# Gate rows computed beside the first products, one chain for q, k and v, and mLSTM written out with its head norm merged

## What is computed

```
proj = x @ w_in    -> qa ka va oa ia fa qkv_b zb beta_b a_b gate_a gate_b
ha   = mlstm(qa, ka, va, i = ia + b_i, f = fa + b_f)        # 4 heads, q and k 128 wide, v 256 wide
       s = (q k^T) * w,  w = exp(decay + i - running max);  h = (s v) / max(|sum s|, exp(-m))
ha   = h * rsqrt(mean(h*h over 256) + 1e-6) * g             # norm of each head
ha   = ha * sigmoid(oa)
qkv  = silu(causal_conv(qkv_b, 4 taps));  hb = gated_delta(l2norm(q), l2norm(k), v, beta, g)
y    = sigmoid(gate_a) * (ha @ w_a) + sigmoid(gate_b) * (hb' @ w_b)
x    = layernorm(ALPHA * x + y @ w_out);  then a gated feed-forward and a second layernorm
```

## Time and profile before

| | us |
|---|---|
| median of 3 runs (4377.66 to 4385.02) | 4377.89 |
| profiled execution | 4381.01 |
| its span, first to last instruction | 4379.2 |
| PE busy | 3860.3 (88%) |
| DVE busy | 1900.5 (43%) |
| ACT busy | 1234.8 (28%) |
| POOL busy | 238.9 (5%) |
| layer 0: gates to the start of branch_a | 1466.37 to 1715.32 |
| layer 1: the same | 2925.25 to 3172.69 |

### The profile page before, as it was taken

The page is one execution under the profiler, slowest core; times in us unless marked ns, Lnnn a source line. Parts: engine busy times, 40 slices in busy tenths (PEclk is TensorE's granted clock), DMA queues, the critical chain, the costliest instruction groups (busy, mean ns, idle before and its releaser), DMA issues. The chain is left out here.

```text
span 4379.2 us, 52698 instructions
## 1 busy us (share of the span) xinstructions
PE 3860.3 (88%) x20305; PEld 3165.7 (72%) x20305; DVE 1900.5 (43%) x2569; ACT 1234.8 (28%) x1839; POOL 238.9 (5%) x300
## 2 busy tenths in 40 slices
PE   7787999989999587998889989958699888898997
PEld 6656999966888364785887778846387588686886
DVE  3365524335433324375444443332436544544333
ACT  2243212234222322323323232223222323323222
POOL 0000000000000000001330000000100033000000
PEclk9888999979999698997999999988799899998999
DMA  2101222211222111220002122212022100122222
GB/s 106 49 9 39 91 93 87 87 33 58 100 96 96 33 58 39 78 95 20 0 0 85 70 93 95 90 46 77 0 96 91 44 1 0 52 100 70 91 94 83
DMA packets 52158, 279.08 MB, mean 64 GB/s; under 512 B 12081, under 2 KB 15161, under 8 KB 23773
## 3 DMA queue, kind: packets, MB, share of 16 engines
q1 hardware_dynamic: 51986, 276.75, 18.6%
HBM read 274.43 MB, written 2.27 MB: 63 GB/s over the span
## 5 line engine op out<-in xcount | busy, mean ns | idle before, releaser
L317 PE MATMUL ps<-xs,ffn_w 128*128 128x512 f32 x2112 | 484.4, 392 | 29.5 <-DVE xs L561 29.5
L317 PEld LDWEIGHTS ps<-xs,ffn_w 128*128 128x128 f32 x2112 | 399.7, 189 | 114.6 <-issue 31.1
L317 PE MATMUL ps<-u,mlp_w 128*128 128x264 f32 (+1 forms) x2880 | 456.2, 321 | 14.8 <-DVE mlp_w L555 10.0
L317 PEld LDWEIGHTS ps<-u,mlp_w 128*128 128x128 f32 x2880 | 417.2, 190 | 53.4 <-issue 15.5
L317 PE MATMUL ps<-hn,mlp_w 128*128 128x264 f32 (+1 forms) x2304 | 363.7, 320 | 0.0
L317 PEld LDWEIGHTS ps<-hn,mlp_w 128*128 128x128 f32 x2304 | 332.4, 188 | 30.4 <-issue 0.5
L317 PE MATMUL ps<-xs,cv_w 128*128 128x512 f32 x1152 | 268.2, 394 | 13.5 <-DVE xs L561 9.8
L317 PEld LDWEIGHTS ps<-xs,cv_w 128*128 128x128 f32 x1152 | 217.5, 190 | 64.2 <-issue 17.7
L317 PE MATMUL ps<-ff,ffn_w 128*128 128x512 f32 x1056 | 240.0, 389 | 0.0
L355 ACT CAST ffn_w<-raw 128x2048 fp32r<-128x2048 f32 (+1 forms) x74 | 124.0, 1676 | 383.2 <-PE ps L317 343.2
L317 PEld LDWEIGHTS ps<-ff,ffn_w 128*128 128x128 f32 x1056 | 198.2, 188 | 41.2
(11 more groups left out here) (422 smaller groups left out, 5497.3 us busy)
## 6 DMA issues: line engine op xcount, KB each, us to landing
raw<-in_w_ffn_up SPq DMA_DIRECT2D x44, 1024.0 KB, 4.9
raw<-in_w_up SPq DMA_DIRECT2D x32, 1024.0 KB, 4.8
raw<-in_w_down SPq DMA_DIRECT2D x32, 1024.0 KB, 4.8
raw<-in_w_conv SPq DMA_DIRECT2D x24, 1024.0 KB, 4.9
raw<-in_w_ffn_down SPq DMA_DIRECT2D x32, 704.0 KB, 4.0
raw<-in_w_mqk SPq DMA_DIRECT2D x10, 1024.0 KB, 5.7
raw<-in_w_mo SPq DMA_DIRECT2D x8, 1024.0 KB, 4.9
mv_raw<-in_w_mv SPq DMA_DIRECT2D x16, 512.0 KB, 6.2
```

The source lines that it names most:

```text
L317: ins = nc.tensor.matmul(bank(u)[:, h, :], w[:, s, wp, k * g.bw + j * P:k * g.bw + (j + 1) * P], g.xs[:, xp, k, h * n:(h + 1) * n], start= ...
```

## The change

- The gates are no stage of their own. A class `Gates` holds their instructions in portions, which `chain` issues on each engine at fixed places (its new argument `beside`): portion -1 before the first product (on ACT and DVE after the splitting of `x`), portion n behind block n. It uses the odd PSUM banks.
- The gate weights stay in a buffer `gates_w` of their own. They are loaded before the layers for layer 0, and at the start of branch_b for the next layer; between, the buffer serves `delta_rule` as its `u`.
- q, k and v are one chain "mqkv" of 4 + 4 blocks. v is a new kind of product, `tokens`: `xs` is the stationary side and 256 columns of weights move, 384 matmuls of 256 columns instead of 192 of 512. Its weights come in the stream like all others.
- `mlstm` is written out for the four heads with two sets of buffers, in an order in which a head's scores are made ahead. q, k, v and a are read where they lie. It makes the head norm too: PE sums the squares of the undivided numerator, and the scaling is 1 / sqrt(sum/256 + 1e-6 * max(..)^2), so division and norm are one reciprocal. `row_norm` "mn" is gone.
- `xs1` stays until the convolution's chain, which no longer splits `x`.

```diff
-        two = [[("w_mqk", 0)], [("w_mo", 0), ("w_branch_a", 0), ("w_ga", 0)], [("w_conv", 0)],
+        two = [[("w_mqk", 0), ("w_mv", 0)], [("w_mo", 0), ("w_branch_a", 0), ("w_ga", 0)], [("w_conv", 0)],
...
+                        if g.evac == "tokens":
+                            for c in range(2):
+                                for k in range(g.kc):
+                                    for e, (wp, xp) in enumerate(PASSES):
+                                        tok = (2 * j + c) * P
+                                        ins = nc.tensor.matmul(
+                                            bank(u)[:, 0, c * BW:(c + 1) * BW], g.xs[:, xp, k, tok:tok + P],
+                                            w[:, s, wp, k * BW:(k + 1) * BW], start=(k == 0 and e == 0),
+                                            stop=(k == g.kc - 1 and e == 2))
...
+                def rest(g, b, pos):
+                    step(g, b, pos)
+                    if beside is not None and isinstance(b, int):
+                        beside.tensor(pe, g.b0 + b)
```

The portions of `Gates` (new code, shortened):

```diff
+    def tensor(self, pe, n):
+        if n == -1:
+            pe.wait_ge(self.w_in, 16 * (self.layer + 1))
...
+        if n == 3:
+            pe.wait_ge(s["a_done"], 1)
+            pe.wait_ge(s["beta_done"], 1)
+            pe.wait_ge(s["gc_done"], NCH)
...
+        if n >= 4:
+            self.spread(pe, 2 * (n - 4))
+            self.spread(pe, 2 * (n - 4) + 1)
...
+    def scalar(self, act, n):
+        if n == 0:      # tanh, sigmoid
...
+        if n == 1:      # exp, exp, abs, exp, ln, ln
...
+        if n == 3:      # exp, two casts
...
+        if n == 4:      # three small exps
...
+        if 5 <= n < 7:
+            self.copy_spread(act, 2 * (n - 5))
+            self.copy_spread(act, 2 * (n - 5) + 1)
+        if n == 7:
+            for j in range(4, 2 * MH):
+                self.copy_spread(act, j)
...
+    def vector(self, dve, n):
+        if n == -1:     # reads the projection, four operations
...
+        if n == 2:      # all running sums and what lies between them
...
+        if n == 4:      # reads the transposes
```

mLSTM, the order on each engine:

```diff
+                scores(0)
+                scores(1)
+                for i in range(MH):
+                    sums(i)
+                    if 1 <= i < MH - 1:
+                        scores(i + 1)
+                    weights_and_squares(i)
...
+                weights(0)
+                weights(1)
+                for i in range(MH):
+                    act.wait_ge(s["summed"], i + 1)
+                    for j in range(2):
+                        if i:
+                            act.wait_ge(s["sq_summed"], i)
+                        nc.scalar.activation(sq[:, j, :], ps[:, 4 + j, :], ACT.Square).then_inc(s["squared"], 1)
+                        nc.scalar.copy(out[:, 2 * i + j, :], ps[:, 4 + j, :]).then_inc(s["copied"], 1)
+                    act.wait_ge(s["den_summed"], i + 1)
+                    nc.scalar.activation(den[:, i % 2, :], ps[:, 7, :], ACT.Abs).then_inc(s["abs_done"], 1)
+                    act.wait_ge(s["bounded"], i + 1)
+                    nc.scalar.activation(den[:, i % 2, :], den[:, i % 2, :], ACT.Square, scale=(EPS * MDV) ** 0.5).then_inc(s["den_squared"], 1)
+                    if i + 2 < MH:
+                        weights(i + 2)
+                    act.wait_ge(s["added"], i + 1)
+                    nc.scalar.activation(inv[:, i % 2, :], inv[:, i % 2, :], ACT.Sqrt, scale=1.0 / MDV).then_inc(s["rooted"], 1)
...
+                args(0)
+                args(1)
+                weigh(0)
+                weigh(1)
+                for i in range(MH):
+                    if i + 2 < MH:
+                        args(i + 2)
+                    if 1 <= i and i + 1 < MH:
+                        weigh(i + 1)
...
+                    dve.wait_ge(s["rooted"], i + 1)
+                    nc.vector.reciprocal(inv[:, i % 2, :], inv[:, i % 2, :]).then_inc(s["inverted"], 1)
```

And in `second_block`:

```diff
-                        gates(nc, ps, x, a, layer, par, ident, ones, sel, m_rows_b, a_cols, g_rows, cols)
-                        chain(nc, ps, ws, "mqk", [dense("qk", xs, KC, D, "act", dst=qk, func=ACT.Copy)], whole=x)
-                        project_tokens(nc, ps, "mv", xs, [c * P for c in range(NCH)], [P] * NCH, a["w_mv"], [layer * 2, layer * 2 + 1],
-                                       SEQ, [v[:, :, j * SEQ:(j + 1) * SEQ] for j in range(2)])
...
-                            chain(nc, ps, ws, "cv", [dense("cv", xs, KC, 3 * D, "conv", dst=qkv, func=ACT.Silu, taps=par[:, CONV_W:CONV_W + 96])], whole=x)
...
+                                chain(nc, ps, ws, "mqkv", [dense("qk", xs, KC, D, "act", dst=qk, func=ACT.Copy),
+                                                           dense("v", xs, KC, D, "tokens", dst=v)], whole=x, beside=beside)
...
+                        chain(nc, ps, ws, "cv", [dense("cv", xs, KC, 3 * D, "conv", dst=qkv, func=ACT.Silu, taps=par[:, CONV_W:CONV_W + 96])])
...
+                                  beside=NextGates(gates_w, gates_in, a["w_gates"], layer))
```

More of the change, by code:

```diff
@@ L185, in __init__, with chain @@
         self.squares, self.inv, self.ones, self.mean = squares, inv, ones, mean
-def chain(nc, ps, ws, name, gemms, whole=None, gain=None, squares=None, room=None):
+def chain(nc, ps, ws, name, gemms, whole=None, gain=None, squares=None, room=None, beside=None):
     halves, n = gemms[0].halves, gemms[0].n
@@ L271, in enter @@
                     eng.wait_ge(sem, count)
+        if beside is not None:
+            beside.open(st)
         with nc.Block() as block:
@@ L275, in _ @@
             def _(sp):
+                if beside is not None:
+                    beside.sync(sp)
                 for i, g in enumerate(gemms):
@@ L335, in _ @@
                         sum_squares(g, i)
-                    rolled(pe, g.n_blocks - 1, g.unroll, lambda b, pos: step(g, b + 1, pos + 1))
+                    if beside is not None:
+                        beside.tensor(pe, g.b0)
+                    rolled(pe, g.n_blocks - 1, g.unroll, lambda b, pos: rest(g, b + 1, pos + 1))
             @block.scalar
@@ L405, in evacuate @@
                             tile(g, b * g.tpb + j, pos, j)
+                    if beside is not None and isinstance(b, int):
+                        beside.scalar(act, g.b0 + b)
                 g = gemms[0]
@@ L421, in _ @@
                             nc.scalar.activation(sq[:, c % 2, :], whole[:, c, :], ACT.Square).then_inc(x_squared, 1)
+                if beside is not None:
+                    beside.scalar(act, -1)
                 for i, g in enumerate(gemms):
@@ L545, in evacuate @@
                         two_parts(g, b, v)
-                    elif g.evac != "act":
+                    elif g.evac not in ("act", "tokens"):
                         for j in range(g.tpb):
                             tile(g, b * g.tpb + j, pos, j)
+                    if beside is not None and isinstance(b, int):
+                        beside.vector(dve, g.b0 + b)
                 g = gemms[0]
@@ L602, in _ @@
                     nc.gpsimd.memset(eps_col[:, :], EPS).then_inc(eps_set, 1)
+                if beside is not None:
+                    beside.gpsimd(pool)
 def project_tokens(nc, ps, name, xs, starts, sizes, w_dram, w_rows, n, dsts, inv=None):
@@ new lines, in sums @@
+                def sums(i):
+                    for n, c in enumerate(order):
+                        pe.wait_ge(s["weighed"], NCH * i + n + 1)
+                        for j in range(2):
+                            if i and c == 0:
+                                pe.wait_ge(s["squared"], 2 * (i - 1) + j + 1)
+                                pe.wait_ge(s["copied"], 2 * (i - 1) + j + 1)
+                            ins = nc.tensor.matmul(ps[:, 4 + j, c * CHUNK:SEQ], v[:, c, i * MDV + j * P:i * MDV + (j + 1) * P],
+                                                   w[:, i % 2, off[c]:off[c] + width[c]], start=(n == 0), stop=(n == NCH - 1))
+                    ins.then_inc(s["summed"], 1)
@@ new lines, in weights_and_squares @@
+                def weights_and_squares(i):
+                    if i:
+                        pe.wait_ge(s["abs_done"], i)
+                    for c in range(NCH):
+                        ins = nc.tensor.matmul(ps[:, 7, c * CHUNK:SEQ], ones, w[:, i % 2, off[c]:off[c] + width[c]],
+                                               start=(c == 0), stop=(c == NCH - 1))
+                    ins.then_inc(s["den_summed"], 1)
+                    for j in range(2):
+                        pe.wait_ge(s["squared"], 2 * i + j + 1)
+                        ins = nc.tensor.matmul(ps[:, 2 * (i % 2), :], ones, sq[:, j, :], start=(j == 0), stop=(j == 1))
+                    ins.then_inc(s["sq_summed"], 1)
@@ new lines, in weights @@
+                def weights(i):
+                    act.wait_ge(s["arg_ready"], i + 1)
+                    if i >= 2:
+                        act.wait_ge(s["den_summed"], i - 1)
```

(13 more changed lines are left out.)

427 lines of the change are left out of this document (221 added, 206 removed).

## The result

The changed kernel takes 4221.04 us, median of four runs (4214.87 to 4225.07), against 4377.77 for the kernel before in the same comparison: a ratio of 0.9637, 95% interval 0.9620 to 0.9654. The forecast of 4217 is 4 us away, inside case A's own range. The profiled execution took 4219.93.

The account below looks back on a forecast made before the run. PE was taken as bound, waiting in chains of small steps in gates and mLSTM; each layer's stretch becomes 111.4 + 56.5 = 167.9 us, saving 160.7 together, 4381.0 to 4220.3, forecast 4217 (3.1 above median), range 4198 to 4250.

Parts of the forecast that it names:

- case A: Whole kernel: the forecast itself, 4217 us, with its own range 4203 to 4231; chance 0.60.
- E: v's matmuls in the chain: held by weight loads, 0.242 us each, 4309 us in all; chance 0.03.
- F: v's matmuls in the chain: 256 columns run at the fp32 rate, 0.43 us each, 4453 us; chance 0.03.
- Margin (a): Chain, block 2: gates portion 1 on ACT, then block 3's cast and DVE's rest, end 0.7 us in time.
- Margin (b): Chain, block 3: portion 2 on DVE (9.2 us), then v's first rest, ready at 10.8 of 11.2 us.
- (c): Chain: portion 3 on ACT, 3 us, delays v's second block to 8 of 11.2 us, still covered.
- C: Chain: helpers late, 4 us at three blocks and one clock fall a layer, 4245 us; chance 0.10.
- The wait: mLSTM, before head 3's sums: PE waits once, 2.5 us, for ACT's exponentials and root, then DVE's reciprocal and products.
- B: Chain and mLSTM: clock falls seven times a layer, 4248 us, shown by a clock under 0.9; chance 0.14.
- "lp": Before layer 0: early gate-weight transfer stands ahead of the parameters this stage waits for; 1.0 us charged once.
- The 0.6 a layer: Convolution's chain: without splitting its input, PE starts at 1.49 us instead of 2.09, saving 0.6 a layer.
- The place of `xs`: Products reading xs: its new SBUF address might alter their rate, worth 0.8 us a layer over 8 tiles, either way.

Follow-up runs that it names:

- the longer helper: Changed kernel with six more ACT operations of 8 x 512 behind the logarithms, ahead of the cast of block 3; 4236.43 us, 0.9663.
- the padded kernel before: Kernel before with 64 unused bytes ahead of the weight buffers of mqk and branch_a; 4388.8 us, 1.0016.
- gates in front: Changed kernel with all portions of the gates issued ahead of the first product; 4264.88 us, 0.9731.
- the first with `xs1` moved: Changed kernel with 32 unused bytes a partition ahead of xs1, its weights not padded; 4214.34 us, 0.9620.

## Why the prediction was right, point by point

- **The chain, 111.4 forecast, 109.9 measured.** Projection 9.0 (10.1), q and k 45.3 (44.8), transposes and end spread 1.1 (1.9), v 4 blocks of 11.5 to 11.6, 46.1 (46.8), spreads 4.5 (4.0), copies behind the last 1.5 (1.9), border 2.1 (1.8). The largest misses are the projection (-1.1) and the transposes (-0.8); the transposes had been seen only at the low clock. The price of 256 columns, 0.121 us a matmul against the 0.122 of 264 columns in the earlier trace rows, kills E and F.
- **Nothing late.** Margin (a) was 0.6 where 0.7 was reckoned. Margin (b) was 2.5 instead of 0.4: DVE's rest for v's first block ends at 1523.20, and PE asks at 1525.7. The step that was off there took portion 2 at its old length of 9.2 us; in the chain it took 7.2, since its last four sums ran without POOL beside them (last section). (c) was 5.9 instead of 3.2. C was priced for several late blocks; the longer helper shows one late block that costs its stall plus 1.5 us and passes nothing on.
- **mLSTM, 56.5 forecast, 56.7 and 56.9 measured.** The wait stands where it was put, 2.80 instead of 2.5. The prediction held that such a wait would leave the clock alone, since only the 5.0 us of the earlier trace rows had cost it; here the sums behind it run at 0.73 and take 1.5 us more. That step failed, but the stage lost only 0.6 by it. Without the fall (the longer helper) PE's last matmul ends 7.45 us before the stage does, the 7.5 of the forecast; with the fall PE ends later, but DVE was the later one there anyway, and 6.5 remain. So the forecast of 56.5 is near because the price of a fall is mostly hidden here. The sign set for B, a clock under 0.9, came in this window (0.89); it holds this fall and the cold first scores, which the sum had.
- **The table loads.** The trace decides for 1.28: the load ends at 1614.02 and the root starts at 1614.03, and nothing idles ahead of the load. The extra 1.38 us that the Trainium skill ("ScalarE: Activation LUTs", "What ACT_TABLE_LOAD costs") adds to each switch is not seen here.
- **"lp" and the convolution.** 1.0 charged, 1.0 measured. The 0.6 a layer is real (PE starts at 1.49 instead of 2.09; the stage 142.9 against 143.6 with the splitting) and was eaten by the next point.
- **The place of `xs`, the step that failed.** The prediction named it as unknown and priced it at 0.8 a layer, from q and k alone. It touches every chain that reads `xs1`: 2.4 us in branch_a and 0.7 in the convolution's chain, 3.1 a layer or 6 in all, the largest error of the sum. q and k, for which it was priced, ran at 5.60 as before.
- **"I am wrong if delta_rule changes by more than 2 us."** It changed by 2.6 in layer 0, and the criterion was a bad one: the same instructions take 243.2 to 248.3 us. The layernorm has the same trait, 25.4 and 23.8 us in the two layers of a kernel that did not touch it (the padded kernel before).

So the mechanism is right, and the total is as near as it is partly by luck. Against the 4220.3 of the forecast for a profiled execution: -2.9 us in the chains, +0.6 in mLSTM, +4.8 in branch_a, +1.4 in the convolution's chain, -3.7 in delta_rule, +0.5 in gn and branch_b, -3.5 and +0.4 in the two layernorms, -1.5 in the chain "ffn" and +3.7 in the first block, together -0.2; measured were 4219.93. The 4 us between 4217 and the median of 4221 come from the profiled executions: the one before lay 3.1 us above its median, the one after 1.1 under.

## What to carry to other kernels

Work of small rows can ride beside products at no cost if each portion ends before the next block's weights are due; read the margin from the helper's last row, because at the first block that misses it the price was the stall and 1.5 us of a fallen clock. When a long-lived operand moves to another address, count every product that reads it, and keep the distance to the weights that it had, here a multiple of 2048 or 4096 bytes. In a helper's queue, put the short operation whose result starts the long one (here a root ahead of a reciprocal) before the bulk work of a later item.

## What the runs showed of the hardware

- DVE's running sums were slower beside POOL's work. The same four sums of 8 x 128 with POOL's subtractions beside them (gates in front; the kernel before has the same 3.33) and without (changed kernel):

```profile
1492.04 1.32 POOL L1796 TENSOR_TENSOR mqkv_parts<-mqkv_r_mneg,mqkv_parts 4x512 fp32r<-4x512 f32 x1 [24.48 <-ACT mqkv_parts L1870]
1492.27 3.33 DVE L1917 TENSOR_TENSOR_SCAN g_rows<-mqkv_g_one,mqkv_g_relu 8x128 f32<-8x128 f32 x4
```

```profile
1519.13 1.36 DVE L1905 TENSOR_TENSOR_SCAN g_rows<-mqkv_g_one,mqkv_g_relu 8x128 f32<-8x128 f32 x4
```

The transposes, for which PE waited in the old gates stage, stand behind these sums. No run varied POOL alone. The Trainium skill ("SBUF — State Buffer", "Who interferes with whom") has a DVE instruction with two SBUF inputs and a GpSimd instruction that reads SBUF contend, the later one being held whole; the rows agree in direction, 2.0 us beside 2.7 us of POOL's work.

- The rate of a product of 512 columns depends on the distance in SBUF between moving and stationary operand: 5.44 us for 24 matmuls at multiples of 4096 bytes, and at odd multiples of 2048, with the weights 64 bytes below one 5.49, 64 above 5.60, 96 below 5.60, 128 above or below 5.57 to 5.60, 160 below 5.62. With 256 moving columns of weights the order is another: 11.16 to 11.58 us for 96 matmuls at 64 below (two kernels with this distance differ), 11.53 and 11.66 at 96 below, 11.78 at a multiple. The numbers are shown, the mechanism isn't. By the same section PE never waits for another reader of SBUF; these rows can't be read against it, since they may be PE's two reads meeting each other, but an engine free of the others is here not free of addresses.
- A wait of 2.80 us before the same sums cost the clock in some executions (sums 6.06 us) and not in others (the kernel with the longer helper, with a granted clock of 1.00 from 1624 to 1632):

```profile
1626.62 4.58 PE L2038 MATMUL ps<-mlstm_w,y 128*128 128x512 f32 x16 [2.80 <-DVE mlstm_w L2106]
```

Eight kernels have this wait, each in two layers. In ten of the 16 layers the sums behind it take 6.04 to 7.66 us, in six 4.58, and in two kernels (gates in front, the first with `xs1` moved) the two layers differ. delta_rule, full of short waits, varies by 5 us. A stage of that kind has no one duration, and a gain of 1 to 2 us can't be read from it. That this also makes the 0.2% by which runs of one kernel differ is likely by size, but wasn't tested.
